# Four transformer layers on one core: wide products in the tiles 4 to 17 of layers 2 and 3, convolution taps on ScalarE and GpSimd, and later waits for the low weight parts

## The reference, cut to what matters

```python
def conv_ffn(h, w_up, conv_w, conv_b, w_down):
    S = h.shape[1]
    u = h @ w_up
    up = jnp.pad(u, ((0, 0), (CONV_WIDTH - 1, 0), (0, 0)))
    c = conv_b
    for j in range(CONV_WIDTH):
        c = c + conv_w[j] * up[:, j:j + S]
    val, gate = jnp.split(c, 2, axis=-1)
    return (jax.nn.silu(gate) * val) @ w_down
```

## Time and profile before

| | |
|---|---|
| median of 3 runs | 1406.19 us |
| the profiled execution | 1407.97 us, its span 1406.2 us |
| TensorE busy | 1353.4 us (96%) |
| VectorE busy | 1006.2 us (72%) |
| ScalarE busy | 734.0 us (52%) |
| GpSimd busy | 96.9 us (7%) |
| chain that ended last | TensorE 80%, VectorE 11%, ScalarE 5% |
| granted TensorE clock, mean | 0.99 |

### The profile page before, as it was taken

The page is one execution under the profiler, slowest core; times in us unless marked ns, Lnnn a source line. Parts: engine busy times, 40 slices in busy tenths (PEclk is TensorE's granted clock), DMA queues, the critical chain, the costliest instruction groups (busy, mean ns, idle before and its releaser), DMA issues.

```text
span 1406.2 us, 23776 instructions
## 1 busy us (share of the span) xinstructions
PE 1353.4 (96%) x9544; PEld 1221.4 (87%) x9544; DVE 1006.2 (72%) x1696; ACT 734.0 (52%) x1216; POOL 96.9 (7%) x79
## 2 busy tenths in 40 slices
PE   9999899999999988999998999999999999999998
PEld 8997698888899867888888998889998998889997
DVE  5677777767859576777785786688778555687776
ACT  4855444444476644444355655554456555654554
POOL 0330000000005100000000011011110000000000
PEclk9999999999999999999999999999999999999999
DMA  8752245555443314655543434435554533545441
GB/s 313 290 190 71 90 167 193 180 192 187 163 180 120 119 61 150 215 197 186 180 152 135 155 115 150 177 143 189 197 193 170 195 111 130 196 164 195 180 180 61
DMA packets 38629, 233.18 MB, mean 166 GB/s; under 512 B 5016, under 2 KB 8808, under 8 KB 12152
## 3 DMA queue, kind: packets, MB, share of 16 engines
q1 hardware_dynamic: 36456, 224.18, 44.4%
q0 software_dynamic: 2064, 7.47, 1.6%
HBM read 230.55 MB, written 1.09 MB: 165 GB/s over the span
## 4 chain that ended last, share of the span: by engine, by line
PE 80%; DVE 11%; ACT 5%; issue 2%; DMA 1%; POOL 0%; DVEq 0%; SPq 0%; ACTq 0%
PE bank L789 15%; PE bank L791 14%; PE bank L790 14%; PE bank L821 10%; PE bank L823 5%; PE bank L797 4%; PE bank L798 4%; PE bank L801 4%; DVE w_lo L616 3%; PE bank L934 1%; ACT w_hi L606 1%; DVE arena L1810 1%; PE bank L1024 1%; PE bank L1059 1%; PE bank L1046 1%
## 5 line engine op out<-in xcount | busy, mean ns | idle before, releaser
L616 DVE TENSOR_TENSOR w_lo<-raw,w_hi 128x1024 fp32r<-128x1024 f32 x404 | 488.0, 1246 | 97.6 <-ACT w_hi L606 93.0
L606 ACT ACTIVATE w_hi<-raw 128x1024 fp32r<-128x1024 f32 x404 | 405.5, 1050 | 120.1 <-PE bank L791 63.5
L789 PE MATMUL bank<-a_both,w_hi 128*128 128x256 f32 x1280 | 368.3, 288 | 6.4 <-DVE w_lo L616 5.7
L790 PE MATMUL bank<-a_both,w_hi 128*128 128x256 f32 x1280 | 364.3, 285 | 0.0
L791 PE MATMUL bank<-a_both,w_lo 128*128 128x256 f32 x1280 | 364.2, 285 | 0.0
L789 PEld LDWEIGHTS bank<-a_both,w_hi 128*128 128x128 f32 x1280 | 247.7, 194 | 11.2 <-issue 8.6
L790 PEld LDWEIGHTS bank<-a_both,w_hi 128*128 128x128 f32 x1280 | 248.0, 194 | 0.5
L791 PEld LDWEIGHTS bank<-a_both,w_lo 128*128 128x128 f32 x1280 | 247.7, 194 | 0.0
L821 PE MATMUL bank<-a_both,w_hi 128*128 128x512 f32 x576 | 204.0, 398 | 0.0
L823 PE MATMUL bank<-a_both,w_lo 128*128 128x256 f32 x576 | 161.7, 281 | 0.0
L821 PEld LDWEIGHTS bank<-a_both,w_hi 128*128 128x128 f32 x576 | 108.2, 188 | 26.8
(11 more groups left out here) (281 smaller groups left out, 2052.7 us busy)
## 6 DMA issues: line engine op xcount, KB each, us to landing
raw<-in_stream SPq DMA_DIRECT2D x201, 1024.0 KB, 4.8
bias_t<-bias_rows SPq DMA_DIRECT2D x6, 512.0 KB, 7.1
heads_buf<-in_w SPq DMA_DIRECT2D x2, 1024.0 KB, 8.4
gains<-in_w SPq DMA_DIRECT2D x2, 1024.0 KB, 10.4
gains<-in_ln_g POOLq DMA_DIRECT2D x4, 512.0 KB, 4.1
gains<-in_ln_b POOLq DMA_DIRECT2D x4, 512.0 KB, 5.6
gains<-in_rms_g POOLq DMA_DIRECT2D x3, 512.0 KB, 3.9
res<-in_xT SPq DMA_DIRECT2D x4, 256.0 KB, 5.4
```

The lines of the kernel that those rows point to most:

```text
L606: act.activation(w_hi[:, i % PARTS, half_tile(h)], raw[:, i % SLOTS, half_tile(h)], ACT.Copy).then_inc(w_hi_done, 1)
L616: dve.tensor_tensor(w_lo[:, i % PARTS, half_tile(h)], raw[:, i % SLOTS, half_tile(h)], w_hi[:, i % PARTS, half_tile(h)].bitcast(F32), ALU. ...
L789: pe.matmul(out, lh, rh, start=first, stop=False)
L790: pe.matmul(out, lh, rl, start=False, stop=False)
```

## The change

Four things change. (1) `apart` now holds in layers 2 and 3 too, for the tiles 4 to 17. (2) In these 28 tiles VectorE reduces both banks to `part_sum`, ScalarE computes tap 2 and bias from there, and also the products of the gate's taps 1 and 0 to `tap_out`; GpSimd adds these two to `cgate`; VectorE adds only the value's two taps. The split of the weights three tiles ahead is cut in two around the SiLU. (3) GpSimd's 16 additions of `neglog` are put behind the gate taps, one for each of the 14 tiles and two at the end. (4) `channels`, `channels_apart`, `tokens` (without a norm) and the down tiles before the tail issue all products with `w_hi` first and those with `w_lo` after them, and wait for each half of `w_hi` and of `w_lo` only where it is used. The tail's `add_rows` is as before. In the diff `conv_apart` is ScalarE's, the part with `val_tap` is VectorE's behind its two reductions, and `gate_taps` is GpSimd's.

```diff
 def apart(l, j):
-    return l < 2 and j >= APART
+    return APART <= j < (FT if l < 2 else FT - 4)
...
             def channels_apart(b, key, c):
                 high, low = [part.rearrange("p (k c) -> p k c", k=KT)[:, :, c * P:(c + 1) * P]
-                             for part in weights(key)]
+                             for part in unsplit(key)]
                 for k in range(KT):
+                    if k % 4 == 0:
+                        wait_part(w_hi_done, key, k // 4)
                     pe.matmul(b, high[:, k, :], a_both[:, k, :, :].rearrange("p i t -> p (i t)"),
                               start=k == 0, stop=False)
+                for k in range(KT):
+                    if k % 4 == 0:
+                        wait_part(w_lo_done, key, k // 4)
                     mm = pe.matmul(b[:, 0:S], low[:, k, :], a_hi[:, k, :], start=False, stop=k == KT - 1)
...
+            def conv_apart(l, j):
+                m = l - 2
+                act.wait_ge(h_done, l * FT + j - 1)
+                for c, dst in enumerate((cval[j % 2], cgate[j % 2])):
+                    wait_drained(act, up_banks(l, j)[c])
+                    ins = act.activation(dst, part_sum[c], ACT.Identity, scale=conv_col[:, m, c * FT + j, 2:3],
+                                         bias=conv_col[:, m, c * FT + j, 3:4])
+                    if c == 0:
+                        ins.then_inc(conv_in, 1)
+                for tap in (1, 0):
+                    act.activation(tap_out[tap][:, 2 - tap:], part_sum[1][:, 0:S - 2 + tap], ACT.Copy,
+                                   scale=conv_col[:, m, FT + j, tap:tap + 1]).then_inc(tap_done, 1)
+                split_half_behind(act, (l, f"up{j}"), split_high, 0)
+                act.wait_ge(gate_conv_done, gates_apart(l, j))
+                act.activation(gate_a[j % 2], cgate[j % 2], ACT.Silu).then_inc(silu_done, 1)
+                split_half_behind(act, (l, f"up{j}"), split_high, 1)
...
+                    else:
+                        dve.wait_ge(conv_in, (l - 2) * FT + j + 1)
+                        wait_drained(dve, up_banks(l, j)[0])
+                        step(val_tap(l, j, 1))
+                        val_tap(l, j, 0).then_inc(conv_done, 1)
+                        split_half_behind(dve, (l, f"up{j}"), split_low, 0)
+                        dve.wait_ge(conv_done, (l - 2) * FT + j + 1)
+                        dve.wait_ge(silu_done, (l - 2) * FT + j + 1)
+                        step(dve.tensor_tensor(full, gate_a[j % 2], cval[j % 2], ALU.mult))
...
+                if l >= 2 and apart(l, j):             # behind h_lo
+                    split_half_behind(dve, (l, f"up{j}"), split_low, 1)
...
+            def gate_taps(l, j):
+                dst = cgate[j % 2]
+                for i, tap in enumerate((1, 0)):
+                    pool.wait_ge(tap_done, 2 * gates_apart(l, j) - 1 + i)
+                    ins = pool.tensor_tensor(dst[:, 2 - tap:], dst[:, 2 - tap:], tap_out[tap][:, 2 - tap:], ALU.add)
+                    if i == 0:
+                        step(ins)
+                ins.then_inc(gate_conv_done, 1)
...
-            for h in range(16):
-                pool.wait_ge(h_done, 2 * FT + 4 + h)
-                ins = pool.tensor_tensor(bias_t[:, 8 + h, :], bias_t[:, 8 + h, :],
-                                         neglog, ALU.add)
+            for j in range(APART, FT - 4):
+                gate_taps(2, j)
+                log_count(2 * HG_HEADS + j - APART)
+            for h in range(24 - 2, 24):
+                ins = log_count(h)
```

More of the change, by code:

```diff
@@ L281, in split_amid @@
 def split_amid(l, j):
-    return l >= 2 and j == FT - 1
+    return l >= 2 and (j == FT - 1 or apart(l, j))
 def norm_after(l):
@@ L422, in build @@
         gain4 = arena[:, 5120:5120 + D]
+        tap_out = [arena[:, 10368 + c * S:10368 + (c + 1) * S] for c in range(2)]
         part_sum = [arena[:, 9856 + c * S:9856 + (c + 1) * S] for c in range(2)]
@@ L502, in build @@
         act_gate = sem("act_gate")
+        tap_done = sem("tap_done")
+        gate_conv_done = sem("gate_conv_done")
         conv_in = sem("conv_in")
@@ L784, in weights, with unsplit, wait_part @@
                 return w_hi[:, i % PARTS, :], w_lo[:, i % PARTS, :]
+            def unsplit(key):
+                i = tile_no[key]
+                return w_hi[:, i % PARTS, :], w_lo[:, i % PARTS, :]
+            def wait_part(done, key, h):
+                pe.wait_ge(done, 2 * tile_no[key] + h + 1)
             def products(out, left, right, first=True, last=True):
@@ L807, in channels @@
             def channels(b, key, c):
-                w = [part.rearrange("p (k c) -> p k c", k=KT) for part in weights(key)]
+                high, low = [part.rearrange("p (k c) -> p k c", k=KT)[:, :, c * P:(c + 1) * P]
+                             for part in unsplit(key)]
+                out = b[:, c * S:(c + 1) * S]
                 for k in range(KT):
-                    mm = products(b[:, c * S:(c + 1) * S], [part[:, k, c * P:(c + 1) * P] for part in w],
-                                  (a_hi[:, k, :], a_lo[:, k, :]), k == 0, k == KT - 1)
+                    if k % 4 == 0:
+                        wait_part(w_hi_done, key, k // 4)
+                    pe.matmul(out, high[:, k, :], a_hi[:, k, :], start=k == 0, stop=False)
+                    pe.matmul(out, high[:, k, :], a_lo[:, k, :], start=False, stop=False)
+                for k in range(KT):
+                    if k % 4 == 0:
+                        wait_part(w_lo_done, key, k // 4)
+                    mm = pe.matmul(out, low[:, k, :], a_hi[:, k, :], start=False, stop=k == KT - 1)
                 return mm
@@ L826, in tokens @@
             def tokens(b, key, tt, norm=None):
-                w = [part.rearrange("p (k c) -> p k c", k=KT) for part in weights(key)]
                 t = slice(tt * P, (tt + 1) * P)
-                tiles = [((a_hi[:, k, t], a_lo[:, k, t]), [part[:, k, :] for part in w]) for k in range(KT)]
                 out = b[:, tt * S:(tt + 1) * S]
                 if norm is None:
+                    high, low = [part.rearrange("p (k c) -> p k c", k=KT) for part in unsplit(key)]
                     for k in range(KT):
-                        mm = products(out, *tiles[k], k == 0, k == KT - 1)
-                    return mm
+                        if k % 4 == 0:
+                            wait_part(w_hi_done, key, k // 4)
+                        pe.matmul(out, a_hi[:, k, t], high[:, k, :], start=k == 0, stop=False)
+                        pe.matmul(out, a_lo[:, k, t], high[:, k, :], start=False, stop=False)
+                    for k in range(KT):
+                        if k % 4 == 0:
+                            wait_part(w_lo_done, key, k // 4)
+                        mm = pe.matmul(out, a_hi[:, k, t], low[:, k, :], start=False, stop=k == KT - 1)
+                    return mm
+                w = [part.rearrange("p (k c) -> p k c", k=KT) for part in weights(key)]
+                tiles = [((a_hi[:, k, t], a_lo[:, k, t]), [part[:, k, :] for part in w]) for k in range(KT)]
                 for q in range(2):
@@ L1106, in add_rows, with add_hidden @@
                     mm.then_inc(rows_used, 1)
+            def add_hidden(l, j):
+                key, (h_high, h_low) = (l, f"down{j}"), hidden(j)
+                high, low = [part.rearrange("p (k c) -> p k c", k=2) for part in unsplit(key)]
+                pieces = [(slice(tt * P, (tt + 1) * P), half_rows(hf), bank[:, 4 + 2 * tt + hf, :])
+                          for tt in range(NT) for hf in range(2)]
+                for n, (t, c, out) in enumerate(pieces):
+                    for kk in range(2):
+                        if n == 0:
+                            wait_part(w_hi_done, key, kk)
+                            pe.wait_ge(h_hi_done, l * FT + 2 * j + kk + 1)
+                        pe.matmul(out, h_high[:, kk, t], high[:, kk, c], start=j == 0 and kk == 0, stop=False)
+                        if n == 0:
+                            pe.wait_ge(h_done, l * FT + 2 * j + kk + 1)
+                        pe.matmul(out, h_low[:, kk, t], high[:, kk, c], start=False, stop=False)
+                for n, (t, c, out) in enumerate(pieces):
+                    for kk in range(2):
+                        if n == 0:
+                            wait_part(w_lo_done, key, kk)
+                        mm = pe.matmul(out, h_high[:, kk, t], low[:, kk, c], start=False, stop=False)
+                mm.then_inc(rows_used, 1)
             def hidden_ready(l, j):
@@ L1167, in feed_forward @@
                             pe.wait_ge(acc_drained, (2 * l + 1) * PIECES)
[L1168 to L1171, removed]
+                        add_hidden(l, j)
                 end = norm_after(l)[1]
```

27 lines of the change are left out of this document (24 added, 3 removed).

## The result

The changed kernel takes 1408.91 us (median of 11 executions, 1407.31 to 1411.86) against 1406.19 of the kernel before (11 executions beside it); the ratio is 1.0021, 95% interval [1.0012, 1.0030]. The forecast was 1403.0. The profiled execution took 1411.86 us, its span 1409.9, which is 3.7 above the span of before; it is the slowest of the 11, so the profiles differ by more than the medians (2.7).

The account below looks back on a forecast made before the run. TensorE was taken to bound the kernel (80% of the chain), with VectorE deciding the change's outcome. Terms -3.3, -1.5, +3.8 and -2.3 summed to -3.3 us: median 1402.9, say 1403, range 1394 to 1415 (8 in 10).

Parts of the forecast that it names:

- Pace in layers 0 and 1: TensorE's 36 wide up tiles in the first two layers: high products first save 0.006 us a k-step, -3.3 us.
- Layer 1's start: First mixer tiles of layer 1: high products run while TensorE would wait for w_lo, -1.5 us, bounds 0 and -5.
- Rival 3: Reordering fails: products keep 0.353 us a k-step, layer 1's levels take back the early start; +1.5 us, 1408; chance 0.17.
- Layer 2: Feed-forward tiles 4 to 17: VectorE's longer serial tile plus the `neglog` additions set the pace, +3.8 us.
- P2: Forecast time of a group (two up tiles, one down) on VectorE in layer 2, with `neglog`: 17.5 us.
- Layer 3: Feed-forward without `neglog`: VectorE's groups get shorter, so tile 21, whose hidden part the tail awaits, comes earlier, -2.3 us.
- P3: Forecast time of a group (two up tiles, one down) on VectorE in layer 3, without `neglog`: 16.6 us.
- c: Time GpSimd's gate additions take from VectorE in each changed tile: 0.2 us, bounds 0 and 1.16.
- the pure rule of who starts first: Shared SBUF port of VectorE and GpSimd: whoever starts first holds it for the whole instruction; alone it gave 16.8 us a group.

## Why the prediction was wrong

Its sum was -3.3; the profiled executions differ by +3.7, and the medians by +2.7.

1. **Pace in layers 0 and 1** (-3.3): right. The pair of tiles took 11.15 (forecast 11.1), the two feed-forwards -1.5 and -1.3, together -2.8.
2. **Layer 1's start** (-1.5, bounds 0 and -5): this term failed, on the far side of its bound. I said 1.7 us of room ahead of the level product at 427.88. The room was there before only as TensorE running late at the 0.50 clock; the VectorE instruction that the level waits for does not depend on the order of TensorE's products there (60.2 us behind the mark in either order, where the clock at the mixer's start is 1.00). So being early bought a wait of 3.49, with the 0.50 clock behind it, and from the level instruction to its end the mixer took 0.3 us more than before, not 1.5 less. The other 1.5 of its +1.8 come from the 0.50 clock at 374 to 378, for which I had no term. Whether that is the chance of one execution or follows from the new order stays open: five of seven profiles of the new order have it and one of four of the old. Rival 3 had the first part right ("levels take back the early start"), and I gave it 0.17. Its sign did not come: the level product started at 426.39, not near 427.9. The true bound was not 0: a wait that moves can cost more than it did where it was.
3. **Layer 2** (+3.8): the mechanism was right, the size was off: the last split came 5.7 later, the feed-forward +6.1. P2 was 17.75, not 17.5. Of that, `neglog` is 0.55 a tile and not 0.45 (its upper bound, 0.58, was nearly the price), and w_hi came a little later than counted (w_lo starts 3.70 behind the first reduction, not 3.55). The last two additions, put behind each other at 1053.47, stretched h_hi and h_lo of tile 17 by another 0.85 (0.72 and 0.85 instead of 0.29 and 0.43), and I had no term for them. From tile 4 to tile 18 VectorE took 125.3 us (935.13 to 1060.44) where I had 122.5; 7 x 0.25 and 0.85 are 2.6 of these 2.8. From tile 18 to the last split it was 0.6 shorter than before (18.9 for 19.45), since the addition at 1057.71 had moved away, which I had not counted. I had booked the move of `neglog` as a gain of 0.55 at tile 4 (935.47; it was 935.13) and as a cover that goes. It weighs more than that: without 14 of the additions the whole change gains 0.34%.
4. **Layer 3** (-2.3): right, -2.0. P3 was 16.69 for 16.6. The gate additions cost c = 0.11 (w_lo 1.33 for 1.22), the rest of the second one; I had taken 0.2. That c came out small is by the same idle 1.28 us that makes the tile long: with w_hi ahead of the taps the additions met w_lo in full. My reason against the pure rule of who starts first was a misread row, as the run with `neglog` held back shows.
5. **Layer 2's mixer**, +0.6 and no term of mine. Between its two marks it took 167.8 to 168.4 us in the four profiles with the old order and 167.7 to 169.2 in the seven with the new, so the +0.6 may be the spread of executions; this stays open.

Most signs I named came: the wait at 408.9 fell to 0.40, VectorE's idle 1.28 is named to w_hi, the chain shifts to VectorE and ScalarE, and nothing waits for the SiLU. Steps 2 and 3 were off by 3.3 and 2.3, together 5.6 of the 7.0 us between forecast and profile.

## What to carry to other kernels

- Where two engines share a port, ask what the busy one runs next when the other asks. GpSimd's addition was free ahead of a reduction from PSUM or an idle VectorE, and cost its full 0.55 us ahead of another instruction with two SBUF inputs (of tile 17's h_hi, with one, it took 0.43). The price depends on the place, not on the addition.
- Work that is sent away to relieve an engine, with a return trip on which that engine's queue waits, can cost more than it takes: two taps on VectorE itself, 0.92 us together, beat four instructions on two little used engines by 0.6% (0.9933 against 0.9992, `neglog` in the same place in both).
- Before a wait is removed, find the next instruction that waits for another engine's own chain. If that chain doesn't move, the wait only moves there. And look up the granted clock before the gain or loss of a stretch is put down to the edit: at the start of layer 1's mixer the same products took 1.5 us more where it was 0.50.

## What the runs showed of the hardware

- An addition on GpSimd (0.74 alone) that is asked for while a w_lo runs waits for its end (1.65 to 1.72 in its row), and the VectorE instruction behind is then longer by 0.54 to 0.55 if it reads two inputs from SBUF; a reduction from PSUM is not longer. The one that has begun is not longer in any of these rows (1.22 and 1.23).
- Layer 1's mixer differs by 3 us (183.5 to 186.6) with where TensorE's clock is 0.50. After the same wait of 3.47 to 3.49 us at the level the clock was 0.50 in six profiles and 1.00 in one. The kernel before itself, on one chip, ran from 1404.2 us at a mean granted clock of 0.993 to 1409.9 at 0.987. One profiled execution lies anywhere in that, so a difference under 3 us between two profiles has to be found in medians too.
